# Prompt attention in a one-layer decoder step: one head at a time, or two heads side by side in the array

## Chip, core and metric

One core of a Trainium2 chip runs the whole program. The metric is device time in microseconds (us) of one execution. The core has a matrix engine (TensorE, PE in the profile, its weight loads PEld), VectorE (DVE), ScalarE (ACT), GpSimd (POOL), and SyncE (SP), which here issues most DMAs. Each engine works through its own instructions in order and waits on semaphores.

## What is computed

The reference is one layer of a decoder for a prompt of 1024 tokens and a group of 64 sample tokens. The part that the change touches is the attention of the prompt, with 8 heads of 64, cut here to its core:

```python
def fox_prompt(q, k, v, logf):            # per block of 128 queries
    c = jnp.cumsum(logf, axis=1).transpose(0, 2, 1)
    s = jnp.einsum('bqhd,bkhd->bhqk', qi, k).astype(jnp.float32) * scale
    s = s + ci[..., :, None] - c[:, :, None, :]
    s = jnp.where(pi[:, None] >= key_pos[None, :], s, -jnp.inf)
    p = jax.nn.softmax(s, axis=-1)
    return jnp.einsum('bhqk,bkhd->bqhd', p.astype(v.dtype), v)
```

Everything is float32. Beside it the same stage of the kernel computes the logits of two gates, `h @ w_in[:, OFF_GA:]`, a product of 1088 tokens by 1024 by 2048, which a later stage uses.

## The kernel before

The program is a chain of stages with a barrier of all engines between them: norm and projections, chunk MLP, **prompt attention with the gate logits** (`stage_prompt_attention`), sample attention over a paged cache, merge, routing, mixture of experts, the end. Only the stage of prompt attention differs.

In it the work is a loop over `n`, 64 steps of one head and one block `i = n % 8` of 128 queries. Keys are causal, so step `n` has `i + 1` blocks of 128 keys, 36 blocks in a head. A step of PE is:

- `scores(n)` (L728): Q of the head (64 rows, one half of the array's rows) is stationary, up to 512 keys stream. One matmul covers four key blocks, a second one the rest. Then one bf16 matmul of 128 columns (L730) adds the causal mask to the last block.
- `gate_half`: four of the eight matmuls (L774) of one piece of the gate logits: 128 output columns by 363 (or 362) tokens. There are 48 pieces, 96 halves, spread as filler: three halves on every two steps.
- `turn(n-1)`: `i + 1` transposes of the exponentials (L740 into bank 4, L747 into bank 5).
- `weigh(n-2)` (L759): for each key block the transposed weights (128 by 128) are stationary and V of the head (64 columns) streams.

DVE adds the forgetting bias and takes the row minimum (`bias`, L847), copies the transposes of bank 5 (L856), and scales the result by the reciprocal of the sum (`scale`, L862 and L864). ACT takes the exponential with its row sum (L815), copies the transposes of bank 4 (L825), and copies gate pieces out of bank 7 (`keep_gate`, L808). Bank 7 is one buffer: the first half of a piece waits until ACT has copied the piece before. `keep_gate` waits until the DMA of the piece four before it has left its slot `RAW[p % 4]`.

The rows of the result lie in `AR`, tokens by features, and after the last step 32 transposes (L795) and 8 copies (L876) turn them into `AT`. At the start SP loads the bias of two heads, two blocks of gate weights (512 columns, 2 MB each), and then writes 9.7 MB of zeros to `y_d`, a buffer of the experts' stage, all on one queue; the outputs of the gates follow on that queue.

A float32 matmul shows as two records of PE in the profile, so 288 matmuls are 576 records. A transpose or a bf16 matmul is one record. The shape in a row says which part of the array is in use: `64*128` is 64 rows by 128 columns, `128*64` all rows by 64 columns.

Of the kernel before, what the change touches and what calls it, by code (L numbers as in the profile page):

```python
# [643 lines left out]
def stage_prompt_attention(nc, c):  # L644
# [5 lines left out]
    AR = view(c, A_AT, NT, WA)  # L650
    AT = view(c, A_AT, NT, NPAIR, P)
    BH = view(c, W_AT, 2, SEQ)
    S = view(c, W_AT + 2 * SEQ, 2, SEQ)
    PT = view(c, W_AT + 4 * SEQ, 2, NP, P)
    zeros = view(c, W_AT + 6 * SEQ, D)
    WG = view(c, W_AT + 2 * WBLK, 2, KD, 512)
    low, total, inv = view(c, T_AT, 2), view(c, T_AT + 2, 4), view(c, T_AT + 6, 4)
    pace = view(c, T_AT + 10, 2 * NP)
# [3 lines left out]
    s_mm, ttr, exps = c.sem("s_mm"), c.sem("s_biased"), c.sem("exps")  # L662
    tr_a, tr_b, ev_a, ev_b = c.sem("p_tr_a"), c.sem("p_tr_b"), c.sem("p_ev_a"), c.sem("p_ev_b")
    pv, rc, norm = c.sem("pv"), c.sem("inv_done"), c.sem("attn_rows")
    at_tr, at_ev = c.sem("at_tr"), c.sem("at_ev")
# [4 lines left out]
    N = H * NP  # L670
    NPIECE = 3 * NCOL

    def late(n):
        return (n // NP) * (NP - 4) + max(n % NP - 4, 0)
# [3 lines left out]

    def halves_before(n):

        return 6 * (n // 4) + (0, 2, 3, 5)[n % 4]

    with nc.Block() as block:
        @block.sync
        def _(sp):
            def load_gates(b):
                sp.dma_start(WG[:, b % 2], c.w_in[:, :, OFF_GA + 512 * b:OFF_GA + 512 * b + 512]
                             ).then_inc(wg_in[b % 2], 16)

            sp.wait_ge(c.scan_out, 16)  # L690
            sp.wait_ge(c.out_rows, 16 * 7)
            for hl in range(2):
                sp.dma_start(BH[:, hl, :], c.cum_d[hl:hl + 1, 0:SEQ].to_broadcast([P, SEQ])).then_inc(bh_in[hl], 16)
            load_gates(0)
            load_gates(1)
            sp.wait_ge(blank, 1)
            sp.dma_start(c.y_d[NUNIT * P:].rearrange("(n p) d -> p n d", p=P),
                         zeros.unsqueeze(1).to_broadcast([P, NOVER, D])).then_inc(c.blank_out, 16)
            for p in range(NPIECE):
                if p in (12, 24):  # L700
                    sp.wait_ge(gate_mm, p)
                    load_gates(p // 12 + 1)
                if p % 6 == 0 and 6 <= p <= 36:
                    head = p // 6 + 1
                    sp.wait_ge(ttr, NP * (head - 1))
                    sp.dma_start(BH[:, head % 2, :], c.cum_d[head:head + 1, 0:SEQ].to_broadcast([P, SEQ])
                                 ).then_inc(bh_in[head % 2], 16)
# [6 lines left out]
        def _(pool):  # L714
            nc.gpsimd.memset(zeros, 0.0).then_inc(blank, 1)

        @block.tensor
        def _(pe):
            mm = nc.tensor.matmul

            def scores(n):
# [8 lines left out]
                last = mm(c.bank[2 * (n % 2) + i // 4][:, (i % 4) * P:(i % 4 + 1) * P], c.ident_b[:],  # L730
                          c.future_b[:], start=False, stop=True, skip_group_check=True)
                last.then_inc(s_mm, 1)

            def turn(n):
                i = n % NP
                pe.wait_ge(exps, n + 1)
                if n >= 1:
                    pe.wait_ge(ev_a, n)
                for k in range(min(i + 1, 4)):
                    last = nc.tensor.transpose(c.bank[4][:, k * P:(k + 1) * P], S[:, n % 2, k * P:(k + 1) * P],  # L740
                                               c.ident[:])
                last.then_inc(tr_a, 1)
                if i >= 4:
                    if late(n) >= 1:
                        pe.wait_ge(ev_b, late(n))
                    for k in range(4, i + 1):
                        last = nc.tensor.transpose(c.bank[5][:, (k - 4) * P:(k - 3) * P],  # L747
                                                   S[:, n % 2, k * P:(k + 1) * P], c.ident[:])
                    last.then_inc(tr_b, 1)

            def weigh(n):
                h, i = n // NP, n % NP
                pe.wait_ge(ev_a, n + 1)
                if n >= 1:
                    pe.wait_ge(norm, n)
# [5 lines left out]
                last.then_inc(pv, 1)  # L761

            def gate_half(g):
# [3 lines left out]
                blk, q = col // 4, col % 4  # L767
                if g % 2 == 0:
                    if p % 12 == 0:
                        pe.wait_ge(wg_in[blk % 2], 16 * (blk // 2 + 1))  # L770
                    if p >= 1:
                        pe.wait_ge(gate_ev, p)
                for k in range(4 * (g % 2), 4 * (g % 2) + 4):
                    last = mm(c.bank[7][:, 0:b - a], WG[:, blk % 2, k, q * P:(q + 1) * P], HT[:, k, a:b],  # L774
                              start=(k == 0), stop=(k == KD - 1))
                if g % 2:
                    last.then_inc(gate_mm, 1)

            for n in range(N + 2):
                if n < N:  # L780
                    scores(n)
                    gate_half(halves_before(n))
                if 1 <= n < N + 1:
                    turn(n - 1)
                if n < N and n % 2 == 0:
                    gate_half(halves_before(n) + 1)
                if n >= 2:
                    weigh(n - 2)
            for t in range(NP):
                if t == 0:  # L790
                    pe.wait_ge(norm, N)
                if t >= 2:
                    pe.wait_ge(at_ev, t - 1)
                for j in range(NPAIR):
                    last = nc.tensor.transpose(c.bank[t % 2][:, j * P:(j + 1) * P], AR[:, t, j * P:(j + 1) * P],  # L795
                                               c.ident[:])
                last.then_inc(at_tr, 1)

        @block.scalar
        def _(act):  # L800
# [8 lines left out]

            for n in range(N + 1):  # L810
                if n < N:
                    i = n % NP
                    act.wait_ge(ttr, n + 1)
# [1549 lines left out]
```

## Time and profile before

| | |
|---|---|
| median of 3 runs | 2228.1 us (2227.83 to 2229.54) |
| the profiled execution | 2225.12 us, its span 2223.5 us |
| stage of prompt attention | 401.7 to 845.7 us of the span |
| PE busy over the span | 1988.0 us, 89% |
| granted TensorE clock, mean | 0.941 |

The span runs from the first to the last recorded instruction. Busy time of PE overlaps between records, since matmuls are pipelined; what a group costs the engine is read from start to start of neighbouring groups in the timeline.

### The profile page before, as it was taken

The page shows a single profiled execution, that of the slowest core. Times are in us where ns is not written, and L with a number is a line of the kernel's source. Part 1 is how long each engine was busy: PE and PEld are TensorE (multiplying, and loading weights), DVE is VectorE, ACT ScalarE, POOL GpSimd, SP SyncE. Part 2 cuts the span into 40 slices and gives each one's busy share as a digit, 9 for nine tenths or more (in the row PEclk, how much of TensorE's full clock was granted, in tenths as well). Part 3 has the DMA queues.
Part 4 walks back from the last instruction along what each step waited for, and adds up shares of the span by engine and source line. Part 5 has one row for each costly group of instructions (what it writes and reads, how often), then busy time and mean ns, then how long its engine had stood idle before and what let it go on. Part 6 is the DMA issues. An engine that isn't in the chain of part 4 may idle for free. (4 is left out here: it accounts for less than half of the span.)

```text
span 2223.5 us, 22907 instructions
## 1 busy us (share of the span) xinstructions
PE 1988.0 (89%) x8429; PEld 1087.9 (49%) x8429; DVE 591.6 (27%) x1287; ACT 303.0 (14%) x489; POOL 190.3 (9%) x280
## 2 busy tenths in 40 slices
PE   8999989799999992877689999479999999994997
PEld 4474445466666662545455555334444444441443
DVE  4201124222222222434223222611111111101776
ACT  1000001122222220323211000000000000000111
POOL 1000013000000001123300000000000000001221
PEclk9989999899999995989789999679999999996999
DMA  6020100701020007999742123279999999993220
GB/s 241 14 78 1 41 20 1 290 30 68 30 72 30 31 24 231 263 317 301 244 167 80 48 76 146 85 285 402 419 418 424 425 419 420 422 370 105 69 79 28
DMA packets 100543, 401.00 MB, mean 180 GB/s; under 512 B 18809, under 2 KB 28090, under 8 KB 87634
## 3 DMA queue, kind: packets, MB, share of 16 engines
q1 hardware_dynamic: 76866, 326.02, 38.4%
q0 software_dynamic: 16496, 56.15, 7.5%
q10 hardware_dynamic: 7072, 17.38, 2.0%
q8 instruction: 68, 1.11, 0.2%
q14 instruction: 41, 0.34, 0.0%
HBM read 353.69 MB, written 45.81 MB: 180 GB/s over the span
## 5 line engine op out<-in xcount | busy, mean ns | idle before, releaser
L1791 PE MATMUL psum<-arena 128*64 128x512 f32 (+1 forms) x1024 | 343.8, 598 | 1.4 <-DVE arena L1881 1.4
L774 PE MATMUL psum<-arena 128*128 128x363 f32 (+1 forms) x768 | 256.7, 477 | 13.9 <-DMA arena<-in_w_in 11.2
L1791 PEld LDWEIGHTS psum<-arena 128*64 128x64 f32 (+1 forms) x1024 | 130.0, 165 | 180.9 <-issue 179.1
L287 PE MATMUL psum<-arena 128*128 128x512 f32 x432 | 189.6, 599 | 0.3 <-DMA arena<-in_w_in 0.3
L774 PEld LDWEIGHTS psum<-arena 128*128 128x128 f32 x768 | 139.7, 192 | 84.6 <-DMA arena<-in_w_in 11.3
L1828 PE MATMUL psum<-arena 128*64 128x512 f32 (+1 forms) x512 | 170.0, 595 | 1.0 <-DVE arena L1895 1.0
L975 PE MATMUL psum<-ident,arena 128*128 128x128 f32 x512 | 80.0, 306 | 66.4 <-DMA arena<-in_cache_k 50.1
L287 PEld LDWEIGHTS psum<-arena 128*128 128x128 f32 x432 | 82.3, 193 | 100.7 <-issue 99.9
L1387 PE MATMUL psum<-arena 128*128 128x512 f32 x288 | 125.7, 594 | 1.6 <-PEq L1244 1.6
L2154 PE MATMUL psum<-arena 128*128 128x512 f32 x288 | 125.1, 592 | 0.0
L1828 PEld LDWEIGHTS psum<-arena 128*64 128x64 f32 (+1 forms) x512 | 66.1, 163 | 101.9 <-issue 101.9
L975 PEld LDWEIGHTS psum<-ident,arena 128*128 128x128 f32 x512 | 63.0, 155 | 87.2 <-DMA arena<-in_cache_k 54.6
L1881 DVE TENSOR_TENSOR arena<-psum,g_moe_rows 128x1024 f32<-128x1024 f32 x24 | 29.4, 1225 | 261.5 <-PE psum L1785 261.5
L2154 PEld LDWEIGHTS psum<-arena 128*128 128x128 f32 x288 | 54.7, 190 | 68.9 <-issue 68.9
L1387 PEld LDWEIGHTS psum<-arena 128*128 128x128 f32 x288 | 54.0, 190 | 66.8 <-issue 66.8
L962 POOL DMA_DIRECT2D arena<-in_cache_v x128 | 68.9, 539 | 196.8 <-PE psum L1025 113.5
L728 PE MATMUL psum<-arena 64*128 64x512 f32 (+2 forms) x192 | 78.8, 517 | 1.1 <-PEq L505 1.1
L815 ACT ACTIVATE arena<-arena 128x128 f32<-128x128 f32 (+3 forms) x64 | 49.6, 775 | 215.0 <-DVE arena L847 215.0
L759 PEld LDWEIGHTS psum<-arena 128*128 128x128 f32 x576 | 71.8, 192 | 9.1 <-issue 1.9
L759 PE MATMUL psum<-arena 128*128 128x64 f32 x576 | 71.4, 269 | 0.7 <-DVE arena L864 0.7
L1266 PE MATMUL psum<-arena 128*128 128x384 f32 x192 | 68.6, 502 | 2.7 <-PEq L116 2.7
L847 DVE CUSTOM_DVE_ANT_0 arena<-psum,arena 128x128 f32<-128x128 f32 (+3 forms) x64 | 48.2, 754 | 69.9 <-issue 69.9
(262 smaller groups left out, 1943.8 us busy)
## 6 DMA issues: line engine op xcount, KB each, us to landing
arena<-in_w_exp_gate SPq DMA_DIRECT2D x32, 2048.0 KB, 13.6
arena<-in_w_exp_up SPq DMA_DIRECT2D x32, 2048.0 KB, 14.1
arena<-in_w_exp_down SPq DMA_DIRECT2D x32, 2048.0 KB, 10.7
arena<-in_cache_v POOLq DMA_DIRECT2D x128, 256.0 KB, 6.6
arena<-in_cache_k SPq DMA_DIRECT2D x128, 256.0 KB, 9.5
arena<-in_w_in SPq DMA_DIRECT2D x9, 2048.0 KB, 10.8
moe_out<-arena ACTq DMA_DIRECT2D x24, 512.0 KB, 11.8
moe_out<-arena SPq DMA_DIRECT2D x1, 9728.0 KB, 38.0
```

What stands on the lines that cost most here:

```text
L287: last = mm(c.bank[4 + r % 3][:, :], HT[:, k, t * P:(t + 1) * P], W[:, n + 1, k, :], start=(k == 0), stop=(k == KD - 1))
L728: mm(c.bank[2 * (n % 2) + half][:, 0:(b - a) * P], QT[r, i, pr, :], KT[r, a:b, pr, :], start=True, stop=False, skip_group_check=True)
L759: last = mm(c.bank[6][:, 0:DH], PT[:, n % 2, k, :], V[:, k, h * DH:(h + 1) * DH], start=(k == 0), stop=(k == i))
L774: last = mm(c.bank[7][:, 0:b - a], WG[:, blk % 2, k, q * P:(q + 1) * P], HT[:, k, a:b], start=(k == 0), stop=(k == KD - 1))
L815: s.activation(S[:, n % 2, 0:w], S[:, n % 2, 0:w], ACT.Exp, bias=low[:, n % 2:n % 2 + 1], scale=-1.0, accum_out=total[:, n % 4:n % 4 + 1]) ...
L962: pool.dma_start(VC[:, ch, g, :], c.cache_v[bass.ds(page * P, P), :]).then_inc(v_in[ch], 16)
L975: last = tp(c.bank[2 + j % 2][:, g * P:(g + 1) * P], KC[:, ch, g, j * P:(j + 1) * P], c.ident[:])
L1266: last = mm(c.bank[p % 4][:, 0:(b - a) * P], UPA[:, k, col * P:(col + 1) * P], AT[:, a:b, k, :], start=(k == 0), stop=(k == KF - 1))
L1387: last = mm(c.bank[2 * (t % 2) + half][:, :], MT[:, k, t * P:(t + 1) * P], WO[:, k, half * 512:half * 512 + 512], start=(k == 0), stop=(k ...
L1791: last = mm(out[rows_, :], XT[:, u % 2, k, rows_], c.ring_tile(LOAD[kind, u, r])[:, k, :], start=(k == 0), stop=(k == KD - 1))
L1828: last = mm(y_ps[rows_, cols], ACT_T[:, k, rows_], c.ring_tile(LOAD["down", u, r])[:, k, cols], start=(k == 0), stop=(k == KF - 1))
L2154: last = mm(gate_ps[:, half * 512:half * 512 + 512], XT[:, t % 2, k, :], c.wpg[half][:, k, :], start=(k == 0), stop=(k == KD - 1))
```

## The change

The stage is rewritten for pairs of heads. There are 32 steps `m`, each of one pair and one block of queries, with a 64-row half of the array for each head in the scores, and a 64-column half for each in the product with V, where V is now stationary and the transposed weights stream. The result then comes out with features in its rows, as `AT` wants it, and the transposes at the end go. Since the sum of a row can no longer be divided out of that result row by row, DVE scales the exponentials before they are transposed. Gate weights come in blocks of 256 columns, three gate halves on every step. The zeros are written from a buffer of 512 columns. DVE's minimum is taken apart for keys 0 to 511 and the rest, and joined by a small instruction. Transposes of the one head go to bank 4 and ACT, of the other to bank 5 and DVE.

```diff
             def scores(n):
-                pr, hl, i = n // (2 * NP), n // NP % 2, n % NP
-                r = slice(hl * DH, (hl + 1) * DH)
-                if n >= 2:
-                    pe.wait_ge(ttr, n - 1)
-                for half in range(i // 4 + 1):
-                    a, b = 4 * half, min(4 * half + 4, i + 1)
-                    mm(c.bank[2 * (n % 2) + half][:, 0:(b - a) * P], QT[r, i, pr, :], KT[r, a:b, pr, :],
-                       start=True, stop=False, skip_group_check=True)
...
+            def scores(m):
+                pr, i = m // NP, m % NP
+                for q, (half, bank, a, b, last) in enumerate(parts(m)):
+                    users = BANK_USER[bank]
+                    at = users.index(parts_before(m) + q)
+                    for hl in range(2):
+                        r = slice(hl * DH, (hl + 1) * DH)
+                        if at >= 1:
+                            pe.wait_ge(ttr, 2 * users[at - 1] + hl + 1)
+                        done = mm(c.bank[bank + hl][:, 0:(b - a) * P], QT[r, i, pr, :], KT[r, a:b, pr, :],
+                                  start=True, stop=not last, skip_group_check=True)
...
+            def turn(m, half):
+                n = parts_before(m) + half
+                k0, k1 = 4 * half, min(4 * half + 4, m % NP + 1)
+                for hl, (tr, ev) in enumerate(((tr_a, ev_a), (tr_b, ev_b))):
+                    pe.wait_ge(scaled, 2 * m + hl + 1)
+                    if n >= 1:
+                        pe.wait_ge(ev, n)
...
-                for k in range(i + 1):
-                    if k == 4:
-                        pe.wait_ge(ev_b, late(n) + 1)
-                    last = mm(c.bank[6][:, 0:DH], PT[:, n % 2, k, :], V[:, k, h * DH:(h + 1) * DH],
-                              start=(k == 0), stop=(k == i))
+                for k in range(i + 1):
+                    for hl in range(2):
+                        r = slice(hl * DH, (hl + 1) * DH)
+                        done = mm(c.bank[6][r, 0:P], V[:, k, (2 * pr + hl) * DH:(2 * pr + hl + 1) * DH],
+                                  PT[:, m % 2, hl, k, :], start=(k == 0), stop=(k == i))
...
-            for n in range(N + 2):
-                if n < N:
-                    scores(n)
-                    gate_half(halves_before(n))
-                if 1 <= n < N + 1:
-                    turn(n - 1)
-                if n < N and n % 2 == 0:
-                    gate_half(halves_before(n) + 1)
-                if n >= 2:
-                    weigh(n - 2)
-            for t in range(NP):
...
+            for m in range(N + 2):
+                if m < N:
+                    scores(m)
+                    gate_half(3 * m)
+                if m % 2 and 2 <= m:
+                    weigh(m - 2)
+                if 1 <= m <= N:
+                    turn(m - 1, 0)
+                if m < N:
+                    gate_half(3 * m + 1)
+                if 1 <= m <= N and (m - 1) % NP >= 4:
+                    turn(m - 1, 1)
+                if m % 2 == 0 and 2 <= m:
+                    weigh(m - 2)
+                if m < N:
+                    gate_half(3 * m + 2)
...
+            for m in range(N + 1):
+                if m < N:
+                    if m % 2 == 0 and m >= 2:
+                        keep_gate(3 * m // 2 - 1)
+                    exp(m, 0)
+                    exp(m, 1)
+                    if m % 2:
+                        keep_gate((3 * m - 1) // 2)
+                if m >= 1:
+                    keep(m - 1, 0)
+                if m < N and m % 2 == 0:
+                    keep_gate(3 * m // 2)
+                if m >= 1 and (m - 1) % NP >= 4:
+                    keep(m - 1, 1)
...
+            def scale(m, hl):
+                w = (m % NP + 1) * P
+                dve.wait_ge(exps, 2 * m + hl + 1)
+                v.reciprocal(inv[:, m % 4, hl:hl + 1], total[:, m % 4, hl:hl + 1]).then_inc(rc, 1)
+                dve.wait_ge(rc, 2 * m + hl + 1)
+                v.tensor_scalar(S[:, m % 2, hl, 0:w], S[:, m % 2, hl, 0:w], inv[:, m % 4, hl:hl + 1], None, ALU.mult
+                                ).then_inc(scaled, 1)
...
+            for m in range(N + 2):
+                if m < N:
+                    bias(m)
+                    scale(m, 0)
+                if 1 <= m <= N:
+                    keep(m - 1, 0)
+                if m < N:
+                    scale(m, 1)
+                if 1 <= m <= N and (m - 1) % NP >= 4:
+                    keep(m - 1, 1)
+                if m >= 2:
+                    keep_out(m - 2)
```

On PE, before, around the last block of queries of head 0 (scores are L728, the mask L730, gates L774, transposes L740 and L747, the product with V L759):

```order
L728 MATMUL psum<-arena 128x512 x2
L730 MATMUL psum<-future_b,ident_b 128x128
L774 MATMUL psum<-arena 128x362 x4
L740 MATMUL psum<-ident,arena 128x128 x4
L747 MATMUL psum<-ident,arena 128x128 x3
L759 MATMUL psum<-arena 128x64 x6
L728 MATMUL psum<-arena 128x128
L730 MATMUL psum<-future_b,ident_b 128x128
L774 MATMUL psum<-arena 128x363 x4
L740 MATMUL psum<-ident,arena 128x128 x4
```

On PE in the changed kernel, around the same block, now of heads 0 and 1 together (scores L744, mask L750, gates L789, transposes L761, the product with V L774, whose output is 64 partitions by 128):

```order
L744 MATMUL psum<-arena 128x512 x4
L750 MATMUL psum<-future_b,ident_b 128x128 x2
L789 MATMUL psum<-arena 128x363 x4
L774 MATMUL psum<-arena 64x128 x12
L761 MATMUL psum<-ident,arena 128x128 x8
L789 MATMUL psum<-arena 128x362 x4
L761 MATMUL psum<-ident,arena 128x128 x6
L789 MATMUL psum<-arena 128x362 x4
L744 MATMUL psum<-arena 128x128 x2
L750 MATMUL psum<-future_b,ident_b 128x128 x2
```

The scores are four matmuls of four key blocks, two for each head, with both masks behind them. The step holds three gate halves of four matmuls where one stood on a step before, and in this odd step the product with V (of step `m - 2`, 12 matmuls for 2 heads by 6 key blocks) stands ahead of the transposes, behind one gate half.

On DVE before, the step of the last block of queries of head 0 (bias with minimum L847, copy of late transposes L856, scaling L862 and L864):

```order
L845 MEMSET arena 128x1
L847 ISA arena<-psum,arena 128x1024
L847 ISA arena 128x1
L856 COPY arena<-psum 128x384
L862 RECIPROCAL arena<-arena 128x1
L864 TENSOR_SCALAR arena<-psum,arena 128x64
```

On DVE in the changed kernel, the end of the same step (bias L876, joining of minima L881, scaling L888 and L890, copies of transposes L899, copy of the result L904):

```order
L874 MEMSET arena 128x1
L876 ISA arena<-psum,arena 128x512
L876 ISA arena 128x1
L881 TENSOR_TENSOR arena<-arena 128x2
L888 RECIPROCAL arena<-arena 128x1
L890 TENSOR_SCALAR arena<-arena 128x1024
L899 COPY arena<-psum 128x512
L888 RECIPROCAL arena<-arena 128x1
L890 TENSOR_SCALAR arena<-arena 128x1024
L899 COPY arena<-psum 128x384
L904 COPY arena<-psum 128x128
```

The bias of both heads stands first, four instructions of 512 columns here, of which the last is shown. The scaling is now of 1024 columns of SBUF and stands ahead of the copies, where it was of 64 columns behind them.

## Rows read from the trace of the kernel before

**Rows 1.** The page: busy time of each engine.

```profile
PE 1988.0 (89%) x8429; PEld 1087.9 (49%) x8429; DVE 591.6 (27%) x1287; ACT 303.0 (14%) x489; POOL 190.3 (9%) x280
```

**Rows 2.** Windows: stretch, length, busy time by engine, granted clock, DMA share, GB/s.

```profile
410.00:420.00 10.00, 6.51 (x16) 3.86 (x16) 0.00 (x0) 0.00 (x0) 0.00 (x0) 0.65 1.05 397
420.00:520.00 100.00, 99.31 (x437) 64.17 (x436) 21.84 (x84) 27.09 (x60) 0.00 (x0) 1.00 0.34 129
```

**Rows 3.** Groups by line, 401 to 846 us: busy, mean ns, idle before.

```profile
L774 PE MATMUL psum<-arena 128*128 128x363 f32 (+1 forms) x768 | 256.7, 477 | 13.9 <-DMA arena<-in_w_in 11.2 <-ACT arena L808 2.8
L728 PE MATMUL psum<-arena 64*128 64x512 f32 (+2 forms) x192 | 78.8, 517 | 1.1 <-PEq L505 1.1
L759 PE MATMUL psum<-arena 128*128 128x64 f32 x576 | 71.4, 269 | 0.7 <-DVE arena L864 0.7
```

**Rows 4.** Timeline of the stage's start: start us, length, engine, line.

```profile
404.22 5.83 SPq L697 DMA_DIRECT2D moe_out<-arena  x1
...
413.49 6.82 PE L774 MATMUL psum<-arena 128*128 128x363 f32 x16 [11.17 <-DMA arena<-in_w_in]
```

**Rows 5.** Timeline of PE in the stage's last steps.

```profile
816.45 1.77 PE L728 MATMUL psum<-arena 64*128 64x512 f32 x4
818.15 0.23 PE L730 MATMUL psum<-future_b,ident_b 128*128 128x128 bf16 x1
...
823.99 1.22 PE L759 MATMUL psum<-arena 128*128 128x64 f32 x10
825.14 1.98 PE L728 MATMUL psum<-arena 64*128 64x512 f32 x4
827.05 0.23 PE L730 MATMUL psum<-future_b,ident_b 128*128 128x128 bf16 x1
...
829.61 0.60 PE L740 MATMUL psum<-ident,arena 128*128 128x128 f32 x4
...
830.37 1.45 PE L759 MATMUL psum<-arena 128*128 128x64 f32 x12
831.66 0.61 PE L740 MATMUL psum<-ident,arena 128*128 128x128 f32 x4
...
837.45 7.21 PE L795 MATMUL psum<-ident,arena 128*128 128x128 f32 x32 [0.58 <-DVE arena L864]
```

**Rows 6.** Timeline of PE in sample attention: four 32-column strips side by side.

```profile
976.67 3.70 PE L1025 MATMUL psum<-arena 128*32 128x128 f32 x128
980.30 0.42 PE L1030 MATMUL psum<-arena 64*32 64x128 f32 x8
```

**Rows 7.** Timeline of PE in the experts: two experts in two column halves.

```profile
1506.51 3.65 PE L1791 MATMUL psum<-arena 128*64 128x512 f32 x16
1510.09 2.41 PE L1828 MATMUL psum<-arena 128*128 128x512 f32 x5
```

**Rows 8.** Groups of DVE and ACT by shape, 320 to 850 us.

```profile
L847 DVE CUSTOM_DVE_ANT_0 arena<-psum,arena 128x512 f32<-128x512 f32 x8 | 5.5, 686 | 5.9 <-issue 5.9
L847 DVE DVE_READ_ACCUMULATOR2_ANT arena<- 128x1 f32 x64 | 5.3, 83 | 0.0
L856 DVE COPY arena<-psum 128x512 f32<-128x512 f32 x8 | 5.5, 692 | 21.0 <-PE psum L747 21.0
L636 DVE TENSOR_SCALAR arena<-arena 128x512 f32<-128x512 f32 x9 | 4.9, 546 | 6.1 <-POOL arena L534 6.1
L808 ACT ACTIVATE arena<-psum 128x363 f32<-128x363 f32 x32 | 15.2, 474 | 54.7 <-PE psum L774 54.7
L815 ACT ACTIVATION_READ_ACCUMULATOR arena<-arena 128x1 f32 x64 | 11.9, 186 | 0.0
L815 ACT ACTIVATE arena<-arena 128x1024 f32<-128x1024 f32 x8 | 9.2, 1151 | 53.1 <-DVE arena L847 53.1
```

**Rows 9.** Timeline: the first instruction of the stage behind this one.

```profile
845.67 0.31 POOL L951 MEMSET arena<- 128x256 f32 x1 [443.05 <-POOLq L683]
```

**Rows 10.** DMA issues, 400 to 460 us: KB each, median us to landing.

```profile
moe_out<-arena SPq DMA_DIRECT2D x1, 9728.0 KB, 38.0
```

More of the change, by code:

```diff
@@ L649, in stage_prompt_attention @@
     V = view(c, V_AT, NT, WA)
-    AR = view(c, A_AT, NT, WA)
     AT = view(c, A_AT, NT, NPAIR, P)
[L652 to L658, printed above, removed]
+    S = view(c, W_AT, 2, 2, SEQ)
+    PT = view(c, W_AT + 4 * SEQ, 2, 2, NP, P)
+    BH = view(c, W_AT + 8 * SEQ, 2, 2, SEQ)
+    WG = view(c, W_AT + 12 * SEQ, 2, KD, 256)
+    low, part = view(c, T_AT, 2, 2), view(c, T_AT + 4, 2, 2)
+    total, inv = view(c, T_AT + 8, 4, 2), view(c, T_AT + 16, 4, 2)
+    pace = view(c, T_AT + 24, 16)
+    zeros = view(c, T_AT + 64, D // 2)
     NRAW = 4
@@ L734, in turn @@
[L734 to L755, printed above, removed]
[L756 to L761 removed]
+            def scores(m):
[9 more added lines that the diff above has]
+                                  start=True, stop=not last, skip_group_check=True)
+                        if not last:
+                            done.then_inc(s_mm, 1)
+                    if last:
+                        for hl in range(2):
+                            mm(c.bank[bank + hl][:, (i - a) * P:(i - a + 1) * P], c.ident_b[:], c.future_b[:],
+                               start=False, stop=True, skip_group_check=True).then_inc(s_mm, 1)
@@ new lines, in keep @@
+            def keep(m, half):
+                n = parts_before(m) + half
+                k0, k1 = 4 * half, min(4 * half + 4, m % NP + 1)
+                act.wait_ge(tr_a, n + 1)
+                if m >= 2:
+                    act.wait_ge(pv, m - 1)
+                s.activation(PT[:, m % 2, 0, k0:k1, :], c.bank[4][:, 0:(k1 - k0) * P].rearrange("p (k n) -> p k n", n=P),
+                             ACT.Copy).then_inc(ev_a, 1)
+            for m in range(N + 1):
[6 more added lines that the diff above has]
+                        keep_gate((3 * m - 1) // 2)
+                if m >= 1:
+                    keep(m - 1, 0)
[3 more added lines that the diff above has]
+                    keep(m - 1, 1)
+                if m == N - 1:
+                    keep_gate(NPIECE - 1)
@@ new lines, in bias @@
+                if m >= 2:
+                    dve.wait_ge(exps, 2 * (m - 1))
+                for q, (half, bank, a, b, _) in enumerate(parts(m)):
+                    for hl in range(2):
+                        n = 2 * (parts_before(m) + q) + hl
+                        dve.wait_ge(s_mm, n + 1)
+                        v.memset(pace[:, n % 16:n % 16 + 1], 0.0)
+                        at = low[:, m % 2, hl:hl + 1] if i < 4 else part[:, half, hl:hl + 1]
+                        done = v.tensor_tensor_reduce(S[:, m % 2, hl, a * P:b * P], c.bank[bank + hl][:, 0:(b - a) * P],
+                                                      BH[:, pr % 2, hl, a * P:b * P], 1.0, 3e38, ALU.add, ALU.min, at)
+                        done.then_inc(ttr, 1)
@@ new lines, in keep, with keep_out @@
+            def keep(m, half):
+                n = parts_before(m) + half
+                k0, k1 = 4 * half, min(4 * half + 4, m % NP + 1)
+                dve.wait_ge(tr_b, n + 1)
+                if m >= 2:
+                    dve.wait_ge(pv, m - 1)
+                v.tensor_copy(PT[:, m % 2, 1, k0:k1, :], c.bank[5][:, 0:(k1 - k0) * P].rearrange("p (k n) -> p k n", n=P)
+                              ).then_inc(ev_b, 1)
+            def keep_out(m):
+                dve.wait_ge(pv, m + 1)
+                v.tensor_copy(AT[:, m % NP, m // NP, :], c.bank[6][:, 0:P]).then_inc(at_ev, 1)
```

156 lines of the change are left out of this document (64 added, 92 removed).

## Prediction, made before the changed kernel ran

> **What bounds the kernel now.** The page gives PE 89% of the span and no other engine over 27% [rows 1]. The windows show that in the stage PE is busy for 99.31 of 100 us at full granted clock, DVE for 22 and ACT for 27 [rows 2]. So the stage lasts as long as PE's own list, plus its start and its end. The groups by line give the list: gate logits, scores, product with V, with 2.8 us of idle behind ACT's copy of gate pieces [rows 3]. Busy times overlap, so I price by start to start.
>
> A scores group of 8 key blocks takes 827.05 - 825.14 = 1.91 us, one of 7 takes 818.15 - 816.45 = 1.70 [rows 5]. That is 0.21 a block and 0.20 besides, the cost of leaving the 64-row shape. The product with V takes 1.15 for 10 records ahead of a scores group, but 831.66 - 830.37 = 1.29 for 12 ahead of transposes, 0.107 a record [rows 5]. The 0.08 over is the way into the 64-row shape. An excursion from the full array and back costs 0.28 to 0.3.
>
> **The change, part by part.**
>
> Scores. 8 heads by 36 blocks by 0.213 (1.91 less 0.20, by 8) are 61.4 us. With both heads at once half is left: -30.7. The trace has no two row halves at work together. Bounds: nothing gained, or the full half. The nearest rows are column strips: two experts in two column halves, 16 records of 512 columns in 1510.09 - 1506.51 = 3.58 us, where one after the other they would take 6.8: a record of 512 columns is half of four blocks' 0.853, so 0.427, by 16 [rows 5, 7]. So halves do overlap, two records of different halves on every 0.45 us, the way out included. I take the full half.
>
> Product with V. Before, 576 records by 0.107 = 61.6 us. There the load of 128 stationary columns paces the engine, since 64 streamed columns would need half of that at the rate of scores (0.213 for two records of 128). Now each key block has two records for each head, 128 columns streamed, 64 stationary. The nearest row is sample attention: 128 records of 128 columns in four strips in 980.30 - 976.67 = 3.63 us, so 32 rounds of four at 0.113 [rows 6]. Two strips have half as many in a round: 288 rounds by 0.113 = 32.5. Worth -29.1. Bounds: halves one after the other, 576 by 0.107 or more, gain nothing; 0.109, the least per 128 columns if the 0.12 us of entry is taken off, gives -30.2.
>
> Excursions. Before 64 for scores. After 32 for scores and 32 for V, whose shape is now a column half. From the experts' rows the way out is 3.58 - 8 by 0.427 = 0.16, less than for rows [rows 7]. So 64 by 0.3 on both sides: 0. If the way out of a column half cost a whole 0.3 by itself, 32 of them would add 5 us.
>
> Masks (64), transposes (288) and gates (96 halves) keep their number and size: 0. They are on PE and hidden by nothing.
>
> End. Before, the last gate half ends at 829.61 and the next stage begins at 845.67, 16.1 us [rows 5, 9]. Of that 8.2 is from L795's start on, and 0.7 + 0.6 are waits for DVE between steps [rows 3, 5]. After, the last steps hold the same kinds as the loop (counted above), plus waits: about 0.5 for copies of the last transposes, 0.6 for DVE's copy of the last result but one (a latency of 0.2 and a copy of 0.29), and 0.5 for the last copy. -9.5 + 1.6 = -7.9.
>
> Start. PE begins the gates at 413.49, held for 11.2 us by gate weights [rows 4]. The queue moves 397 GB/s there [rows 2], and the block in front is 1 MB in place of 2: 1 MB / 397 = 2.6 us earlier. -2.6. Packets half as long could take more for each byte: between 0 and -2.6, and I take -2.6, since the row's transfers are of gate weights too.
>
> New waits. Bank 7 is single, so PE's next piece waits for ACT's `keep_gate`, which now stands behind two exponentials on odd `m`. For `m = 7`, counted from the first score's arrival: DVE has four biases of 512 columns, each 0.69, 0.08 for the read of the minimum [rows 8] and 0.06 for the memset ahead (an estimate below that read), 0.83, together 3.3; the joining 0.15 (an estimate, two such reads); two exponentials of 1024 columns, 1.15 and some 0.1 each before the next [rows 8], 2.5; the gate copy 0.47; five semaphores 0.3, my estimate. 6.7 us. PE meanwhile has the rest of the scores and masks, 1.1 (the second four blocks overlap), one gate half 2.5, the product of step 5, 6 by 0.226 + 0.3 = 1.7, eight transposes 0.9 (seven take 830.37 - 829.61 = 0.76 [rows 5]): 6.2. A wait of 0.5. For `m = 5` and `m = 3` the same sum gives 0 to 0.1, on even `m` the copy has another gate half as cover; where it has only a short product (i = 2) the latency of the copy shows, 0.25. The reset of a pair adds 0.2. That is about 1.1 on each of 4 pairs, and 1.2 on the first two pieces, which have nothing behind them: 5.6. Without this cover the copies would cost 0.75 each, 36 us for 48.
> DMA: SP issues the zeros at 404.22 and they land 38 us later, at 442 [rows 4, 10]; the gate outputs queue behind them. The byte count of all that is ahead stays within 1 MB. Piece 4 needs slot 0 free; its copy comes at about 411 + 10 halves by 2.5 + some 6 of attention = 442. So ACT waits 0 to 3 us there, I take 2. Sum 7.6, against 3.6 before (2.8 idle plus the latencies under the modelled ends): +4.0.
>
> DVE gains work that nothing waits for as long as it is under PE: a step of `m = 7` is 3.3 + 0.15 + a wait of 1.3 + two scalings of 1024 (0.55 for 512 in L636, so 1.1 each) with two reciprocals at 0.15, 2.5 + copies 1.3 + 0.3 = 8.9 us [rows 8]. PE's step: scores 2.1, three gate halves 7.5, 14 transposes 1.5, V 1.7: 12.8.
>
> Sum: -30.7 - 29.1 + 0 - 7.9 - 2.6 + 4.0 = -66.3. The profiled execution of 2225.1 would come to 2158.8. The median of the runs is 3.0 above it, so 2228.1 - 66.3 = **2162**.
>
> **The rivals.**
>
> A: one of the packings does not overlap. For: no row has two row halves of the array at work; both would write 128 partitions each, where column strips share them. Against: column strips overlap almost perfectly [rows 6, 7]. Price: about 30 less gain, 2191 to 2193. The Trainium skill ("TensorE: Matmul & The Clock Gate", Measured speedup vs the span model) gives 3.07 times for four row tiles, not four. By that ratio two halves would gain 1.54 times, the scores fall to 39.9 in place of 30.7 and the time would be 2171, an estimate from that page; no row here shows it.
>
> B: the chain DVE - ACT - DVE takes PE's place as the bound in the late steps. Its links are long in series (6.7 us above against 6.2), and each further 0.1 us on one of eight DVE instructions is paid on odd steps from `m = 3` on. If the four biases cost 1.0 each and not 0.83, `m = 5` and `m = 7` pay 0.7 each, the lighter odd steps 0.3: 8 us more in all. If every link grew by a third, `m = 7` would pay 2.7, `m = 5` 1.6, the others 1 each, 6 in a pair less the 1.1 counted: 20 in all. 2170 to 2182. For: PE idles behind L808 today [rows 3]. Against: DVE and ACT are idle for three quarters [rows 2]. The Trainium skill ("TensorEngine Tiling (Array Packing)", PSUM Bottleneck) warns that tiling does not speed up evacuation. This is that warning as a mechanism of this kernel.
>
> C, slower: PE's clock falls. The granted clock is 0.65 in the window with the 11 us wait for gate weights, and 1.00 in the ones without [rows 2]. The list after is some 356 us, of which the low level (1.2 GHz) doubles what falls under it. If waits let the clock be low for 66 us' worth of that list, the gain is gone, 2228; past that it is slower, with 80 at 2242. The place would be late odd steps, the only ones that wait again and again. Against: waits of 0.5 us between stretches of over 5 us of work, as today, where 2.8 us of them left 1.00.
>
> **How the numbers follow.** Forecast, 2153 to 2170: 0.72 (the least from waits of 3 in place of 7.6 and 0.109 a round, -72, and the clock of single runs; the most from 12 of waits). B beyond that to 2184: 0.12. A: 0.11. C: 0.02, and 0.01 for no gain from an unseen cause. Below 2153: 0.02. The range 2152 to 2184 leaves out A, C and the low end, 0.16. What tells from no change here is 0.2%, 4.5 us: faster 0.96, same 0.01, slower 0.03.
>
> **What the profile will show.** Records of scores and of V in pairs some ns apart, 0.21 us for two key blocks of a pair of heads; scores group of i = 7 from start to mask near 1.9 for both heads; V near 0.11 for a pair of records; gates begin near 411; PE's idle behind the gate copy near 0.5 at `m` = 7, 15, 23, 31, under 8 us in sum; ACT held once near 442 by a DMA of gate outputs; the stage from 401.7 to near 779. The granted clock stays at 1.00 from 420 on. The forecast is wrong if the two records of a pair come one after the other (A), if idle under gates passes 20 us (B), or if another stage moves: nothing but this stage is changed.

## The result and the profile after

The changed kernel takes 2153.57 us (median of 4 runs, 2150.29 to 2163.09), the kernel before 2227.97 (4 runs, 2225.51 to 2229.54). The ratio is 0.9674, 95% interval 0.9642 to 0.9707: 74.4 us faster by the medians. The forecast was 2162, in a range of 2152 to 2184. The profiled execution took 2151.96 us, its span is 2150.3, and 73.2 us are gone from the span of before.

First the page, engine busy times, to be set beside [rows 1]:

```profile
PE 1923.0 (89%) x8397; PEld 1031.1 (48%) x8397; DVE 620.6 (29%) x1439; ACT 289.1 (13%) x473; POOL 191.0 (9%) x280
```

Groups by line over the stage (401 to 780 us), the answer to [rows 3]:

```profile
L789 PE MATMUL psum<-arena 128*128 128x363 f32 (+1 forms) x768 | 253.5, 474 | 10.1 <-DMA arena<-in_w_in 8.4 <-ACT arena L820 1.7
L744 PE MATMUL psum<-arena 64*128 64x512 f32 (+3 forms) x192 | 40.0, 521 | 1.1 <-PEq L505 1.1
L774 PE MATMUL psum<-arena 128*64 128x128 f32 x576 | 38.5, 278 | 0.5 <-DVE arena L904 0.5
```

The numbers of records are the same, 192 and 576, and the mean length of one is hardly changed, 521 and 278 ns. What halved is the time in which any of them runs: 78.8 to 40.0 and 71.4 to 38.5 us. Idle behind the gate copy (L820) is 1.7 us, it was 2.8.

The timeline of PE in the stage's last steps, the answer to [rows 5]:

```profile
756.38 1.99 PE L744 MATMUL psum<-arena 64*128 64x512 f32 x8
758.30 0.28 PE L750 MATMUL psum<-future_b,ident_b 128*128 128x128 bf16 x2
758.42 2.66 PE L789 MATMUL psum<-arena 128*128 128x363 f32 x8
761.01 1.53 PE L774 MATMUL psum<-arena 128*64 128x128 f32 x24
762.47 1.09 PE L761 MATMUL psum<-ident,arena 128*128 128x128 f32 x8
763.40 2.60 PE L789 MATMUL psum<-arena 128*128 128x362 f32 x8
765.84 0.82 PE L761 MATMUL psum<-ident,arena 128*128 128x128 f32 x6
...
768.93 1.04 PE L761 MATMUL psum<-ident,arena 128*128 128x128 f32 x8
770.31 1.16 PE L761 MATMUL psum<-ident,arena 128*128 128x128 f32 x8 [0.34 <-ACT arena L836]
771.40 1.75 PE L774 MATMUL psum<-arena 128*64 128x128 f32 x28
773.63 1.97 PE L774 MATMUL psum<-arena 128*64 128x128 f32 x32 [0.48 <-DVE arena L904]
```

Eight key blocks of two heads take 758.30 - 756.38 = 1.92 us, where one head took 1.91. The product with V of 24 records takes 762.47 - 761.01 = 1.46. Between the last gate half (768.93) and the next stage there are 7.3 us, with two waits.

The timeline of the stage's two ends (PE's first scores, its first gates, and the first instruction of the stage behind), the answer to [rows 4, 9]:

```profile
407.55 0.80 PE L744 MATMUL psum<-arena 64*128 64x128 f32 x4 [1.05 <-PEq L505]
...
417.03 6.55 PE L789 MATMUL psum<-arena 128*128 128x363 f32 x16 [8.35 <-DMA arena<-in_w_in]
...
776.21 0.31 POOL L992 MEMSET arena<- 128x256 f32 x1 [368.17 <-POOLq L692]
```

The stage takes 776.21 - 407.55 = 368.7 us. Before it took 443.96 (401.71 to 845.67). That is 75.3 less, so the gain is in the stage, to within what the other stages vary from run to run.

One part of the stage varies too: the first 16 records of the gates, two halves, take 6.55 us here and took 6.82 before, at a granted clock of 0.78 and 0.75. So a second measure is used below, the **body** of the stage, from the end of these 16 records to the next stage. Before it is 845.67 - (413.49 + 6.82) = 425.4 us, after it is 776.21 - (417.03 + 6.55) = 352.6 us: 72.7 less.

Windows of after (length; busy time by engine; granted clock, DMA share, GB/s), the answer to [rows 2]:

```profile
410.00:420.00 10.00, 2.97 (x5) 1.84 (x6) 1.37 (x10) 0.88 (x4) 0.00 (x0) 0.51 1.05 341
420.00:520.00 100.00, 98.89 (x509) 60.64 (x508) 33.14 (x136) 25.89 (x63) 0.00 (x0) 1.00 0.44 162
```

PE is busy and at its upper level (2.4 GHz) from 420 us on; the gates begin at 417.03, and over their first 16 records it is 0.78. DVE rises from 22 to 33 us in 100 and has room.

### The profile page after: what moved, and what is told of

Same layout as the page of the kernel before. It is cut to its first block and busy times, and to the rows that moved or that the text cites. A ratio compares the mean times of both kernels' runs of the same rounds, so it can differ in the third digit from the quotient of the medians.

```text
span 2150.3 us, 23048 instructions
## 1 busy us (share of the span) xinstructions
PE 1923.0 (89%) x8397; PEld 1031.1 (48%) x8397; DVE 620.6 (29%) x1439; ACT 289.1 (13%) x473; POOL 191.0 (9%) x280
## 5 line engine op out<-in xcount | busy, mean ns | idle before, releaser
L789 PE MATMUL psum<-arena 128*128 128x363 f32 (+1 forms) x768 | 253.5, 474 | 10.1 <-DMA arena<-in_w_in 8.4
L287 PE MATMUL psum<-arena 128*128 128x512 f32 x432 | 190.3, 600 | 0.0
L789 PEld LDWEIGHTS psum<-arena 128*128 128x128 f32 x768 | 139.5, 191 | 83.5 <-DMA arena<-in_w_in 8.6
L287 PEld LDWEIGHTS psum<-arena 128*128 128x128 f32 x432 | 82.7, 193 | 100.5 <-issue 100.5
L1428 PE MATMUL psum<-arena 128*128 128x512 f32 x288 | 125.7, 594 | 1.6 <-PEq L1285 1.6
L2195 PE MATMUL psum<-arena 128*128 128x512 f32 x288 | 125.1, 592 | 0.0
L2195 PEld LDWEIGHTS psum<-arena 128*128 128x128 f32 x288 | 54.7, 190 | 68.9 <-issue 68.9
L1428 PEld LDWEIGHTS psum<-arena 128*128 128x128 f32 x288 | 54.0, 190 | 66.8 <-issue 66.8
L1307 PE MATMUL psum<-arena 128*128 128x384 f32 x192 | 67.5, 495 | 2.7 <-PEq L116 2.7
L827 ACT ACTIVATE arena<-arena 128x128 f32<-128x128 f32 (+7 forms) x64 | 49.1, 768 | 141.3 <-DVE arena L881 80.2
L571 PE MATMUL psum<-arena 128*128 128x512 f32 x144 | 65.2, 608 | 1.8 <-PEq L189 1.1
L1801 POOL DMA_INDIRECT arena<-moe_in,arena x24 | 22.7, 946 | 492.5 <-PE psum L1826 450.1
L1313 PE MATMUL psum<-arena 128*128 128x384 f32 x192 | 65.8, 486 | 0.0
L1196 DVE COPY arena<-psum 128x512 f32<-128x512 f32 x64 | 44.2, 690 | 74.1 <-PE psum L1016 74.1
## 6 DMA issues: line engine op xcount, KB each, us to landing
moe_out<-arena SPq DMA_DIRECT2D x1, 9728.0 KB, 32.1
```

Source lines behind the costliest of these rows:

```text
L287: last = mm(c.bank[4 + r % 3][:, :], HT[:, k, t * P:(t + 1) * P], W[:, n + 1, k, :], start=(k == 0), stop=(k == KD - 1))
L571: last = mm(c.bank[t % 2][:, :], HT[:, k, t * P:(t + 1) * P], W[:, 0, k, :], start=(k == 0), stop=(k == KD - 1))
L789: done = mm(c.bank[7][:, 0:b - a], WG[:, blk % 2, k, q * P:(q + 1) * P], HT[:, k, a:b], start=(k == 0), stop=(k == KD - 1))
L827: s.activation(S[:, m % 2, hl, 0:w], S[:, m % 2, hl, 0:w], ACT.Exp, bias=low[:, m % 2, hl:hl + 1], scale=-1.0, accum_out=total[:, m % 4, h ...
L1307: last = mm(c.bank[p % 4][:, 0:(b - a) * P], UPA[:, k, col * P:(col + 1) * P], AT[:, a:b, k, :], start=(k == 0), stop=(k == KF - 1))
L1313: last = mm(c.bank[4 + p % 4][:, 0:(b - a) * P], UPB[:, k, col * P:(col + 1) * P], BT[:, a:b, k, :], start=(k == 0), stop=(k == KF - 1))
```

## The experiments

Six edited kernels ran, one of them twice, and the changed kernel a second time. They ran in two series, and in both the kernel before takes a little less than in the comparison above, 2222.73 and 2222.78 us. The changed kernel ran again in the second series: 2151.36 us (5 runs, 2144.6 to 2155.3), ratio 0.9671, 0.9644 to 0.9698. Since whole programs of one kernel spread by 0.5%, the stage's own length, from the first scores to the next stage, is the finer measure: 368.7 us in the first trace of the changed kernel, and 370.0 in the second:

```profile
403.21 0.80 PE L744 MATMUL psum<-arena 64*128 64x128 f32 x4 [1.05 <-PEq L505]
...
412.57 8.06 PE L789 MATMUL psum<-arena 128*128 128x363 f32 x16 [8.23 <-DMA arena<-in_w_in]
...
773.25 0.31 POOL L992 MEMSET arena<- 128x256 f32 x1 [369.56 <-POOLq L692]
```

The difference lies in the first 16 gate records, 8.06 us at a granted clock of 0.63 against 6.55 at 0.78. The body is 773.25 - (412.57 + 8.06) = 352.6 us in both traces. So each experiment is read by both measures: the stage against 368.7 carries up to 1.5 us of this clock, the body against 352.6 does not.

> The changed kernel itself, for a time on the same chip as the three others of this call. Every theory says 0.967 of the kernel before, with a narrower interval; the stage from the first scores to the next stage 368.7 us as in its first trace.

### Both heads' scores in one row half

```diff
                     for hl in range(2):
-                        r = slice(hl * DH, (hl + 1) * DH)
+                        r = slice(0, DH)
                         if at >= 1:
```

> Both heads' scores read rows 0 to 63 of Q and K, so head 1 of each pair gets the scores of head 0 and the two matmuls share one row half of the array; number, size and order are those of the changed kernel. If the gain of the scores is that two row halves work at once, the stage gets longer by 288 key blocks x 0.107 = 30.7 us: 2184 us, with a group of eight key blocks for both heads at 3.6 us in place of 1.92. The rival, that the gain comes from having 32 groups in place of 64 (half the ways out of the 64-row shape), says no change: 2154.

It takes 2183.82 us (ratio to before 0.9823, 0.9792 to 0.9853). In the timeline of its PE, the group of eight key blocks and the ends of the stage:

```profile
402.23 0.68 PE L744 MATMUL psum<-arena 64*128 64x128 f32 x4 [1.05 <-PEq L505]
...
411.81 7.70 PE L789 MATMUL psum<-arena 128*128 128x363 f32 x16 [8.68 <-DMA arena<-in_w_in]
...
780.59 3.70 PE L744 MATMUL psum<-arena 64*128 64x512 f32 x8
784.22 0.29 PE L750 MATMUL psum<-future_b,ident_b 128*128 128x128 bf16 x2
...
802.13 0.31 POOL L992 MEMSET arena<- 128x256 f32 x1 [399.41 <-POOLq L692]
```

The group takes 3.63 us in place of 1.92, and the stage 399.9 in place of 368.7: +31.2, where +30.7 was expected. The body is 382.6, +30.0. The two row halves do work at once, and that is the 30 us: the rival, by which the number of groups is the gain, falls. Fewer groups are worth something small by themselves, since two groups of before take 2 x 1.91 = 3.82 and this one 3.63, about 0.2 for each of 32.

### V of both heads in one column half

```diff
-                for k in range(i + 1):
-                    for hl in range(2):
-                        r = slice(hl * DH, (hl + 1) * DH)
-                        done = mm(c.bank[6][r, 0:P], V[:, k, (2 * pr + hl) * DH:(2 * pr + hl + 1) * DH],
+                for hl in range(2):
+                    for k in range(i + 1):
+                        done = mm(c.bank[6][0:DH, hl * P:(hl + 1) * P], V[:, k, (2 * pr + hl) * DH:(2 * pr + hl + 1) * DH],
                                   PT[:, m % 2, hl, k, :], start=(k == 0), stop=(k == i))
...
-                v.tensor_copy(AT[:, m % NP, m // NP, :], c.bank[6][:, 0:P]).then_inc(at_ev, 1)
+                v.tensor_copy(AT[0:DH, m % NP, m // NP, :], c.bank[6][0:DH, 0:P])
+                v.tensor_copy(AT[DH:P, m % NP, m // NP, :], c.bank[6][0:DH, P:2 * P]).then_inc(at_ev, 1)
```

> V of both heads stands in the same 64 columns of the array, one head after the other, and DVE puts the two results in place with two copies. V stays stationary with 64 columns and the weights stream. If the gain of this product is that two column halves work at once, 288 rounds of 0.109 become 576 of 0.109: +31.4 us, 2185. The rival, that the gain comes from loading 64 stationary columns in place of 128, says 0.107 for a record fell to 0.055 by itself, so at most a few us are lost here: under 2160.

It takes 2181.77 us (ratio 0.9807, 0.9786 to 0.9828). In its timeline:

```profile
405.59 0.80 PE L744 MATMUL psum<-arena 64*128 64x128 f32 x4 [1.05 <-PEq L505]
...
414.76 6.70 PE L788 MATMUL psum<-arena 128*128 128x363 f32 x16 [8.04 <-DMA arena<-in_w_in]
...
784.73 2.83 PE L773 MATMUL psum<-arena 128*64 128x128 f32 x24
787.50 1.09 PE L761 MATMUL psum<-ident,arena 128*128 128x128 f32 x8
...
805.03 0.31 POOL L992 MEMSET arena<- 128x256 f32 x1 [398.96 <-POOLq L692]
```

24 records take 2.77 us in place of 1.46, and the stage 399.4: +30.8, expected +31.4. The body is 383.6, +30.9. The lighter weight load alone gives nothing: 24 records with 64 stationary and 128 streamed columns take 2.77 us here, and 24 with 128 stationary and 64 streamed take 2.62 in the kernel with V as before, below.

### Both edits at once

> Both earlier edits at once: both heads' scores from rows 0 to 63 (head 1 gets head 0's), and V of both heads in one column half, one after the other. If the two packings add up, the stage takes 368.7 + 31.2 + 30.8 = 430.7 us, still 13 us under the 444.0 of the kernel before, which is what the end without transposes (about 9), the shorter first block (2.3) and fewer waits are worth. If without packing the stage is no better than before, 444.

It takes 2213.01 us (10 runs, 2206.03 to 2220.83; ratio 0.9953, 0.9933 to 0.9973). Its stage:

```profile
401.96 0.68 PE L744 MATMUL psum<-arena 64*128 64x128 f32 x4 [1.05 <-PEq L505]
...
411.77 7.75 PE L788 MATMUL psum<-arena 128*128 128x363 f32 x16 [8.91 <-DMA arena<-in_w_in]
...
833.05 0.31 POOL L992 MEMSET arena<- 128x256 f32 x1 [430.60 <-POOLq L692]
```

431.1 us against an expected 430.7, +62.4. By the body, 413.5, it is +60.9, which is 30.0 and 30.9 added up: the two packings do not depend on each other. Of the 72.7 us that the body lost, 11.8 are left for the rest; the start, ahead of the body, makes up the other 2.6 of the 75.3.

### The product with V as before

```diff
-                for k in range(i + 1):
-                    for hl in range(2):
-                        r = slice(hl * DH, (hl + 1) * DH)
-                        done = mm(c.bank[6][r, 0:P], V[:, k, (2 * pr + hl) * DH:(2 * pr + hl + 1) * DH],
-                                  PT[:, m % 2, hl, k, :], start=(k == 0), stop=(k == i))
+                for hl in range(2):
+                    for k in range(i + 1):
+                        done = mm(c.bank[6][:, hl * DH:(hl + 1) * DH], PT[:, m % 2, hl, k, :],
+                                  V[:, k, (2 * pr + hl) * DH:(2 * pr + hl + 1) * DH], start=(k == 0), stop=(k == i))
...
+            for t in range(NP):
...
+                for j in range(NPAIR):
+                    done = nc.tensor.transpose(c.bank[t % 2][:, j * P:(j + 1) * P], AR[:, t, j * P:(j + 1) * P],
+                                               c.ident[:])
```

> The product with V as in the kernel before (transposed weights stationary over the full array, 64 columns of V stream), with the 32 transposes at the end; all else as changed. Theory: +30.2 us for 576 records at 0.107 against 288 rounds at 0.109, -8 us for 32 excursions into the column half that go, +8.8 us for the end: +31 us, 2185. The rival, that excursions cost nothing here since scores lie next to them, says +39: 2193.

It takes 2183.18 us (ratio 0.982, 0.9796 to 0.9845). Its stage, and a product with V behind a gate half:

```profile
401.81 0.49 PE L746 MATMUL psum<-arena 64*128 64x128 f32 x4 [1.05 <-PEq L505]
...
411.25 7.88 PE L790 MATMUL psum<-arena 128*128 128x363 f32 x16 [8.73 <-DMA arena<-in_w_in]
...
772.39 2.66 PE L790 MATMUL psum<-arena 128*128 128x363 f32 x8
774.89 2.79 PE L775 MATMUL psum<-arena 128*128 128x64 f32 x24
777.51 1.04 PE L763 MATMUL psum<-ident,arena 128*128 128x128 f32 x8
...
800.73 0.31 POOL L1006 MEMSET arena<- 128x256 f32 x1 [398.43 <-POOLq L694]
```

398.9 us, +30.2, expected +31. The body is 381.6, +29.0. The rival's +39 is out by both. So the swap of operands with its packing is worth 29 to 30 us net: about 39 gained from the streams and the end, less 9 to 10 for 32 excursions into the column half. The rows of one group show an excursion directly. The gate half ahead of V takes 774.89 - 772.39 = 2.50 us here and 761.01 - 758.42 = 2.59 in the changed kernel, and the changed kernel's 1.46 us for 12 rounds is 0.15 more than 12 x 0.109: 0.24 us in all, 7.7 for 32.

### The first gate block loaded a stage earlier

```diff
 # stage_mlp, SP:
+            c.first_gates = c.sem("first_gates")
+            sp.dma_start(view(c, W_AT + 12 * SEQ + KD * 256, KD, 256), c.w_in[:, :, OFF_GA:OFF_GA + 256]
+                         ).then_inc(c.first_gates, 16)
 # stage_prompt_attention:
-                sp.dma_start(WG[:, b % 2], c.w_in[:, :, OFF_GA + 256 * b:OFF_GA + 256 * b + 256]
+                sp.dma_start(WG[:, (b + 1) % 2], c.w_in[:, :, OFF_GA + 256 * b:OFF_GA + 256 * b + 256]
...
-            load_gates(0)
...
-                    if p % PER_BLOCK == 0:
-                        pe.wait_ge(wg_in[blk % 2], 16 * (blk // 2 + 1))
+                    if p == 0:
+                        pe.wait_ge(c.first_gates, 16)
+                    elif p % PER_BLOCK == 0:
+                        pe.wait_ge(wg_in[blk % 2], 16 * ((blk + 1) // 2))
```

> The first block of gate weights is loaded in the stage before, into the 2048 columns that this stage leaves free, and the two slots change places. PE waits 8.4 us for that block in the changed kernel. Theory: nothing else is late there, the bias of the first pair lands 6.5 us into the stage, behind two gate halves: 7 to 8 us faster, 2146. The rival: the first exponential and so the first copy of a gate piece still wait for the bias, and PE works its first halves at the low clock anyway, so 3 us or less: 2151.

> The kernel with the first gate block loaded a stage earlier, against the changed kernel on one chip. In the first trace its stage took 362.8 us against 368.7, so the theory says 5.8 us under the run beside it, 0.27%, about what five rounds can tell. The rival says that a stage whose time depends on the clock gives it back: no difference in the median, the stage still 362.8.

The first time it took 2149.0 us (ratio 0.9657, 0.9636 to 0.9678), beside the changed kernel 2145.22 (5 runs, 2142.89 to 2150.82; ratio 0.966, 0.9633 to 0.9686) against 2151.36. The stage takes 362.8 and 363.0 us. In the timeline of the first:

```profile
406.14 0.80 PE L746 MATMUL psum<-arena 64*128 64x128 f32 x4 [1.05 <-PEq L505]
...
407.06 7.30 PE L793 MATMUL psum<-arena 128*128 128x363 f32 x16
...
442.76 0.47 ACT L824 ACTIVATE arena<-psum 128x363 f32<-128x363 f32 x1 [2.00 <-DMA gate_logits<-arena]
...
443.28 5.13 PE L793 MATMUL psum<-arena 128*128 128x362 f32 x16 [1.71 <-ACT arena L824]
...
768.98 0.31 POOL L996 MEMSET arena<- 128x256 f32 x1 [362.35 <-POOLq L695]
```

PE starts its gates 0.9 us into the stage, not 9.5, and 5.8 to 7 of the 8.6 us are kept. Beside the first 16 gate records (7.30 us here, 6.55 and 8.06 in the two traces of the changed kernel), what is given back is one new wait: idle behind the gate copy is 3.4 us in all, 1.7 more than in the changed kernel, and 1.71 of it stand at 443.28. There PE waits for ACT's copy of the fifth gate piece, and ACT waited 2.00 us for the DMA of the first piece to leave its slot `RAW[0]`. That DMA, issued at 414.90, stands behind the zeros in the queue: they land at 442.2 (32.3 us after their issue at 409.87), it lands at 442.7, and ACT had come to the copy at 440.8. In the second trace of this kernel the same wait is 2.31 us on ACT and 2.02 on PE. So the zeros, which the changed kernel just escapes, become the next limit of the start. The stage is faster in both traces. In whole programs the intervals of the two ratios overlap, so 6 us by the medians is the likely size, not a settled one.

### A longer bias instruction

```diff
                         v.memset(pace[:, n % 16:n % 16 + 1], 0.0)
+                        if n >= 1:
+                            dve.wait_ge(idled, n)
+                        v.memset(idle, 0.0).then_inc(idled, 1)
```

> Each bias instruction of DVE is preceded by a memset of 448 columns, about 0.43 us, which nothing reads: 1.7 us more on the chain from scores to exponentials at four or more key blocks, 0.9 below. Walk through the odd steps with the durations seen in the trace after (0.62 for a bias of 512 columns): the copy of the gate piece is 0.1 us early for eight key blocks, 0.5 to 1 early for the others, so PE waits some 11 us more in all and the stage takes 380. If the chain were already the bound the whole 1.7 would show on each of 16 heavy steps and half of it on the light ones: a stage of 409. If the slack is ample: 369.

It takes 2168.21 us (ratio 0.9751, 0.9721 to 0.978), its stage 388.0 (406.82 to 794.79). Its group of PE's gate matmuls over the stage:

```profile
L790 PE MATMUL psum<-arena 128*128 128x363 f32 (+1 forms) x768 | 256.2, 478 | 22.2 <-ACT arena L821 14.0 <-DMA arena<-in_w_in 8.1
```

And in its timeline the first gates, and two places where PE waits:

```profile
416.09 8.02 PE L790 MATMUL psum<-arena 128*128 128x363 f32 x16 [8.15 <-DMA arena<-in_w_in]
...
765.86 2.60 PE L790 MATMUL psum<-arena 128*128 128x363 f32 x8
...
768.89 0.42 PEld L762 LDWEIGHTS psum<-ident,arena 128*128 128x128 f32 x4 [1.00 <-DVE arena L894]
...
768.92 0.63 PE L762 MATMUL psum<-ident,arena 128*128 128x128 f32 x4 [0.45 <-ACT arena L837]
...
779.46 1.09 PE L762 MATMUL psum<-ident,arena 128*128 128x128 f32 x8
...
781.88 2.70 PE L790 MATMUL psum<-arena 128*128 128x362 f32 x8 [1.33 <-ACT arena L821]
```

PE's idle behind the gate copy is 14.0 us, where it is 1.7 in both traces of the changed kernel: +12.3, about what the walk gave. The memset is 0.43 us, 41 us on 96 biases. The stage takes 19.3 us more than in the first trace of the changed kernel (17.9 against the second, whose first gates ran at about the same clock; 18.1 by the body), expected 11. Neither ample slack (369) nor a chain that is the bound throughout (409) is right.

The walk missed two things. PE also comes too early to four groups of transposes, where its weight load waits 1.00 us for the scaling (L894) and the matmul behind it 0.45. These two rows are one wait; from start to start the transposes come 768.92 - 765.86 = 3.06 us after the gate half, where 2.44 is usual (765.84 - 763.40), so 0.6 late. And idle time is counted from the ends of the records before, which the profile only models (each reaches past the start of the next record). That hides part of each wait ahead of a gate half: 781.88 - 779.46 = 2.42 us in place of 0.93 is 1.49 late, where the row gives 1.33. The starts of all 96 gate halves, beside those of the second trace of the changed kernel, are late by 2.6 us in sum over the four transposes and by 15.4 elsewhere, 18.0 together.

## Why the prediction was right

The forecast's mechanism held for both packings, the end and the start, and one term, the new waits, was wrong in sign. The sum was 8 us short of the gain (66.3 against 74.4), 9 by the stage. The range held the time by luck as much as by skill: 72 was the most that the prediction could get out of its terms, 2153.57 lies within the range by an allowance for the spread of single runs, and the 2151.36 of the second series would lie just below 2152, beside a kernel before that is 5 us faster as well.

- **Scores, -30.7.** 30.0 by the body of the kernel with one row half, 31.2 by its stage. Rival A, that one packing does not overlap, is out. The Trainium skill ("TensorE: Matmul & The Clock Gate", Measured speedup vs the span model) gives 3.07 times for four row tiles; here two row halves of float32 gain 3.63 / 1.92 = 1.89 times in a group with its way out, and 1.71 us of streams in place of 3.42, two times, without it. The estimate of 2171 that hung on that ratio did not come about.
- **Product with V, -29.1.** 30.9 by one column half (body; 30.8 by the stage). The 0.113 for a round held an entry; it is 0.109, (2.77 - 1.46) / 12 from the twelve records that no longer run beside others in that kernel.
- **Excursions, 0.** 32 into the row half fell away and 32 into the column half came. The latter cost 0.24 each by the rows of one group, against 0.28 to 0.3, so the net is a gain of 1 to 2 us.
- **End, -7.9.** In the terms of the prediction 8.2 and two waits of 0.67 and 0.58, 9.5 together, became waits of 0.34 and 0.48 and 0.61 from the end of the last product (775.60) to the next stage, 1.4 together: -8.1. From the last gate half on it is 16.1 to 7.3 us, -8.8, which holds some of what V gained too.
- **Start, -2.6.** 11.8 to 9.5 us from first scores to first gates, -2.3, and 0.3 less for the first 16 records.
- **New waits, +4.0: this term was wrong in sign.** 75.3 less 30.0, 30.9, 8.1, 2.3 and 0.3 leaves 3.7 of gain. PE's idle behind the gate copy is 1.7 us, before it was 2.8, which is 1.1 of the 3.7; I had 7.6. The masks give 0.6 (two every 0.12 us, 758.42 - 758.30, where one took 0.07, 818.22 - 818.15, by 32 and 64), the excursions 1 to 2, and the rest, up to 1 us, is not traced. Of the 7.6, the part on the first two pieces is 0.56 + 0.34 (I had 1.2) and the one at i = 2 is 0.19 in each of 4 pairs (0.25), both real. The 0.5 at `m` = 7, 15, 23, 31 and the 2 us behind a DMA of gate outputs did not come. For the first the durations that I carried over were too long. The timeline of DVE and ACT in the last step:

```profile
757.71 0.69 DVE L876 CUSTOM_DVE_ANT_0 arena<-psum,arena 128x512 f32<-128x512 f32 x1
758.32 0.08 DVE L876 DVE_READ_ACCUMULATOR2_ANT arena<- 128x1 f32 x1
758.33 0.69 DVE L876 CUSTOM_DVE_ANT_0 arena<-psum,arena 128x512 f32<-128x512 f32 x1
...
761.97 0.75 DVE L890 TENSOR_SCALAR arena<-arena 128x1024 f32<-128x1024 f32 x1
...
762.77 0.45 ACT L820 ACTIVATE arena<-psum 128x363 f32<-128x363 f32 x1
```

Biases follow each other at 758.33 - 757.71 = 0.62 us, since one's start lies under the end and the read of the other. I had added up the instruction, the read and the memset to 0.83. Four times the 0.21 between them is 0.84 us, more than the 0.5 by which `m = 7` was to be late. Here the gate copy ends at 763.22 and PE takes the bank at 763.40, right behind its transposes. The scaling takes 0.75 us for 1024 columns, not 1.1.

The zeros were no hindrance: 9.7 MB landed 32.1 us after their issue at 414.57, at 446.6, and ACT came to the fifth gate piece at 449.88. But the margin is about 3 us, and the kernel with the first gate block loaded earlier falls on the other side of it (ACT held for 2.00 and 2.31 us). That part of the prediction had the right mechanism and was off by a few microseconds in time.

- **Rival B** is real as a mechanism, and nearer than I thought: 0.43 us on each bias costs 18 us. Of 41 us added on DVE nearly half reaches PE. The Trainium skill ("TensorEngine Tiling (Array Packing)", PSUM Bottleneck) warns that evacuation may become the next limit after tiling; with PE's step halved in two of its parts this kernel has some tenths of a microsecond of slack, and the longer bias shows the limit.
- **Rival C** did not come: the granted clock is 1.00 from 420 us on. At the start it is 0.51, with the wait for gate weights and for the bias, and the first 16 gate records ran at 0.63 to 0.78 from trace to trace, worth up to 1.5 us.

## What to carry to other kernels

Two matmuls in opposite halves of the array, rows or columns, in float32 too, run as one when they stand next to each other in the program; price them at one, and the way into and out of the half at 0.25 to 0.3 us for each group. Other distances in the program were not tried. When an operand has 64 columns, making it the stationary one was worth nothing by itself here, only the second column half was. For a chain of instructions on one engine, count from start to start: adding shown durations made a wait out of a slack here. And look next at what evacuates: 0.43 us on each bias took a quarter of the gain.

## What the runs showed of the hardware that was not expected

DVE's scaling of SBUF by a scalar of each row goes at 0.52 ns a column ((0.75 - 0.28) us by 896 columns, from widths 1024 and 128), half of the 1.04 of a copy out of PSUM. For 512 columns it takes 487 ns, whereas the trace of before had 546 in a stage where GpSimd works beside it. The cause of that difference was not tried.

The stages that the change does not touch vary from execution to execution. The chunk MLP ahead, which has the same code in both kernels, took 95.4 us in the trace of before and 99.6 in that of after, where the clock was granted 0.50 in the 8 us around the stages' border:

```profile
402.00:410.00 8.00, 4.97 (x23) 3.70 (x22) 2.68 (x4) 1.28 (x1) 0.53 (x1) 0.50 0.18 46
```

Sample attention behind took between 269 and 278 us in the traces of all these kernels. These differences are as large as the spread of 0.5% between runs of one kernel, and they are why a gain of 6 us shows in the stage and not surely in the whole.
